# A two-layer decoder trunk on one core: the expert loop rewritten, with two-pass matmuls for experts of at most 64 tokens

## The reference

```python
def moe_swiglu(h, w_router, w_gu, w_down):
    logits = (h @ w_router).astype(jnp.float32)
    top_vals, top_idx = lax.top_k(logits, TOP_K)
    gates = jax.nn.softmax(top_vals, axis=-1)
    comb = jnp.sum(jax.nn.one_hot(top_idx, N_EXPERTS, dtype=jnp.float32) * gates[..., None],
                   axis=-2).astype(h.dtype)
    y = jnp.zeros_like(h)
    for e in range(N_EXPERTS):
        y = y + comb[..., e:e + 1] * swiglu(h, w_gu[e], w_down[e])
    return y
```

## Time and profile before

| | before |
|---|---|
| median of 3 runs | 1827.52 us (1825.49 to 1830.34) |
| profiled execution, span | 1824.5 us |
| TensorE, VectorE, ScalarE busy | 1688.0, 1270.3, 1020.9 us |
| moved by DMA | 452.27 MB, mean 248 GB/s |
| expert stage | from the first gather at 632.84 us to the end |

### The profile page before, as it was taken

How to read it: one execution, slowest core, us unless ns; L and a number is a source line. 1 busy time by engine, 2 the same in 40 slices (tenths; PEclk the granted TensorE clock), 3 DMA queues, 4 the chain that set the end, 5 groups by cost and what they waited for, 6 DMA issues and landing times.

```text
span 1824.5 us, 21578 instructions
## 1 busy us (share of the span) xinstructions
PE 1688.0 (93%) x7605; PEld 1391.9 (76%) x7606; DVE 1270.3 (70%) x1081; ACT 1020.9 (56%) x883; POOL 9.6 (1%) x22
## 2 busy tenths in 40 slices
PE   7999999999997889979979979979998899799996
PEld 5887778887786778868868868868886688688785
DVE  6645644454697568868878878856654788788886
ACT  4344433433476367757757757644544577577674
POOL 0000000000000000000000000000000000000000
PEclk9999999999998799989989989989998999899999
DMA  9553455555421269979979979946665699799893
GB/s 350 193 199 111 143 189 194 185 192 180 167 96 44 79 230 370 348 252 369 350 254 369 349 255 374 333 164 228 223 215 177 222 378 340 257 368 349 318 367 135
DMA packets 191716, 452.27 MB, mean 248 GB/s; under 512 B 8492, under 2 KB 8892, under 8 KB 191420
## 3 DMA queue, kind: packets, MB, share of 16 engines
q1 hardware_dynamic: 189212, 445.35, 69.2%
q10 hardware_dynamic: 2336, 4.78, 0.7%
HBM read 449.06 MB, written 1.05 MB: 247 GB/s over the span
## 4 chain that ended last, share of the span: by engine, by line
PE 88%; DVE 7%; issue 3%; ACT 1%; DMA 0%; DVEq 0%; POOL 0%; SPq 0%; ACTq 0%; POOLq 0%
PE bank L1218 28%; PE bank L1219 28%; PE bank L1222 26%; DVE y L996 2%; DVE wlo L739 2%; PE bank L1374 2%; PE bank L1483 1%; PE bank L1484 1%; DMA raw<-in_ret_w_in 0%; DVE z L751 0%; PE bank L1464 0%; PE bank L1262 0%; ACT whi L414 0%; DVE res L1160 0%; PE bank L1442 0%
## 5 line engine op out<-in xcount | busy, mean ns | idle before, releaser
L739 DVE TENSOR_TENSOR wlo<-raw,whi 128x2048 fp32r<-128x2048 f32 x422 | 964.3, 2290 | 340.4 <-ACT whi L414 340.1
L414 ACT ACTIVATE whi<-raw 128x2048 fp32r<-128x2048 f32 x422 | 807.7, 1916 | 423.0 <-PE bank L1222 366.3
L1218 PE MATMUL bank<-whi,xh 128*128 128x512 f32 x1520 | 607.9, 400 | 83.4 <-issue 62.4
L1219 PE MATMUL bank<-wlo,xh 128*128 128x512 f32 x1520 | 601.0, 395 | 0.0
L1222 PE MATMUL bank<-whi,xl 128*128 128x512 f32 x1408 | 556.5, 395 | 0.0
L1218 PEld LDWEIGHTS bank<-whi,xh 128*128 128x128 f32 x1520 | 291.8, 192 | 146.6 <-issue 71.1
L1219 PEld LDWEIGHTS bank<-wlo,xh 128*128 128x128 f32 x1520 | 291.3, 192 | 59.1
L1222 PEld LDWEIGHTS bank<-whi,xl 128*128 128x128 f32 x1408 | 269.8, 192 | 57.7
L1218 PE MATMUL bank<-whi,hTh 128*128 128x512 f32 x616 | 242.3, 393 | 4.4 <-DVE hTl L921 2.5
L1219 PE MATMUL bank<-wlo,hTh 128*128 128x512 f32 x616 | 242.6, 394 | 0.0
L1222 PE MATMUL bank<-whi,hTl 128*128 128x512 f32 x560 | 218.6, 390 | 0.0
(11 more groups left out here) (184 smaller groups left out, 792.1 us busy)
## 6 DMA issues: line engine op xcount, KB each, us to landing
raw<-in_moe_w_gu SPq DMA_DIRECT2D x224, 1024.0 KB, 6.4
raw<-in_moe_w_down SPq DMA_DIRECT2D x112, 1024.0 KB, 6.6
raw<-in_ffn_w_gu SPq DMA_DIRECT2D x28, 1024.0 KB, 5.1
raw<-in_ret_w_in SPq DMA_DIRECT2D x24, 1024.0 KB, 6.0
raw<-in_ffn_w_down SPq DMA_DIRECT2D x14, 1024.0 KB, 4.9
raw<-in_conv_w_pw SPq DMA_DIRECT2D x12, 1024.0 KB, 5.0
raw<-in_ret_w_out SPq DMA_DIRECT2D x8, 1024.0 KB, 4.8
res<-in_x SPq DMA_DIRECT2D x2, 512.0 KB, 4.6
```

The costliest lines, as they stand in the source:

```text
L414: nc.scalar.activation(whi[base % SPLIT][:, :], raw[base % RAW][:, :], ACT.Copy).then_inc(hi_done, 1)
L739: nc.vector.tensor_tensor(wlo[base % SPLIT][:, :], raw[base % RAW][:, :], whi[base % SPLIT][:, :].bitcast(f32), ALU.subtract).then_inc(lo_ ...
L1218: nc.tensor.matmul(dst, ah, bh, start=start, stop=False)
L1219: last = nc.tensor.matmul(dst, ah, bl, start=False, stop=stop and al is None)
```

## The change

Forms are now decided by tile and by 64 tokens: an expert is (HALF_FULL), (FULL), (FULL, HALF_FULL) or (FULL, FULL), for up to 64, 128, 192 and 256 tokens. In a half-full tile the tokens stand twice in the tile, so that the slice across the boundary between high part and remainder (`xmix`, `hTmix`) holds 64 columns of each; up and down blocks take two matmuls with it (`half_product`), gates take three. The two halves are added by the turn (with `fold` in place of the identity) and by the scatter. ScalarE's `low`, VectorE's `fold` and the buffers `glow` and `ulow` are gone.

Each engine has one loop over all eight experts, whose body holds each form once: ACT and DVE with one or two tiles, TensorE with four kinds. Gather of the next expert's first tile comes ahead of the last down rows; its evacuation, the evacuation of the last result, the scatter and the accumulation come inside the next expert, the scatter between its gate and up blocks. For expert 0 these work on a result weighted by zero (column 0 of `comb`), and after the loop one scatter and one accumulation follow. A second tile is gathered ahead of the expert's gates, and scattered and accumulated (`accumulate2`) at its end. The gates of an expert no longer run ahead of the last down rows of the one before. GpSimd has four memsets more.

```diff
-        xh = at("xh", [P, DC, SEQ], f32r)
-        xl = at("xl", [P, DC, SEQ], f32r)
+        xx = at("xx", [P, DC, TILES, 2 * P], f32r)
+        xh, xl, xmix = xx[:, :, :, 0:P], xx[:, :, :, P:2 * P], xx[:, :, :, HALF:HALF + P]
...
+            nc.gpsimd.memset(zeros[:, :].bitcast(f32), 0.0).then_inc(moe_set, 1)
+            nc.gpsimd.memset(onehotT[:, :, :].bitcast(f32), 0.0).then_inc(moe_set, 1)
+            nc.gpsimd.memset(comb[:, :, 0:1], 0.0).then_inc(moe_set, 1)
+            nc.gpsimd.memset(slot[:, NE, :, :], -1.0).then_inc(moe_set, 1)
...
+            def expert(e, tiles):
+                six, done = STEPS * e, STEPS * e + STEPS
+                xh_gathered(e)
+                if tiles == 2:
+                    xh_gathered2(wide_before(act, e))
+                hi(B_MOE + 1, six)
+                y_hi(B_MOE + 6 * six)
+                hi(B_MOE + 2, six)
+                hi(B_MOE + 3, six)
+                silu(done, B_MOE + 2 + 6 * six, tiles)
+                hi(B_MOE + 4, six)
+                hi(B_MOE + 5, six)
+                ohT_evac(e, tiles)
+                with act.Fori(0, STEPS - 1) as i:
...
+                hTh_evac(done + STEPS, tiles)
+                if tiles == 2:
+                    y_hi2(B_MOE + MOE_BLOCKS + 6 * six)
...
             def build_onehot(e):
-                for i, (a, b) in enumerate(((0, P), (0, HALF), (HALF, P))):
-                    at_ = (0, P, P)[i]
-                    for t in range(TILES):
-                        last = nc.vector.tensor_scalar(onehot[:, t, at_ + a:at_ + b], iota[:, a:b],
-                                                       slot[:, i, t, bass.ds(e, 1)], None, ALU.is_equal)
+                for h in range(2):
+                    for n in range(2 * TILES):
+                        at_ = n % 2 * P + h * HALF
+                        last = nc.vector.tensor_scalar(onehot[:, n // 2, at_:at_ + HALF], iota[:, h * HALF:(h + 1) * HALF],
+                                                       slot[:, bass.ds(e, 1), n, h], None, ALU.is_equal)
...
+            def expert(e, tiles):
+                six, done = STEPS * e, STEPS * e + STEPS
+                n2 = wide_before(dve, e) if tiles == 2 else None
+                xl_gathered(e, tiles, n2)
+                lo(B_MOE + 1, six)
+                y_lo(e)
+                lo(B_MOE + 2, six)
+                lo(B_MOE + 3, six)
+                accumulate(e)
+                hidden(done, B_MOE + 4 + 6 * six, tiles)
                 dve.wait_ge(ohT_ps, e + 1)
                 build_onehot(e + 1)
...
                 lo(B_MOE + 4, six)
                 lo(B_MOE + 5, six)
+                with dve.Fori(0, STEPS - 1) as i:
+                    hTl_evac(done + 1 + i, tiles)
+                    for b in range(6, 10):
+                        lo(B_MOE + b, six + i)
+                    hidden(done + 1 + i, B_MOE + 8 + 6 * (six + i), tiles)
+                    lo(B_MOE + 10, six + i)
+                    lo(B_MOE + 11, six + i)
+                hTl_evac(done + STEPS, tiles)
+                if tiles == 2:
+                    y_lo2(n2)
+                    accumulate2(e, n2)
...
+            def half_product(dst, both, bh, bl, start, stop):
+                nc.tensor.matmul(dst, both, bh, start=start, stop=False)
+                return nc.tensor.matmul(dst, both, bl, start=False, stop=stop)
...
+            def expert(e, kinds):
+                six, done, tiles = STEPS * e, STEPS * e + STEPS, len(kinds)
+                gates = (FULL,) * tiles
+                n2 = wide_before(pe, e) if tiles == 2 else None
+                if tiles == 2:
+                    gather(e, 1).then_inc(gather2_ps, 1)
+                pe.wait_ge(xel_done, e + 1)
+                columns(B_MOE, bank[0:2], 0, kinds=gates, six=six)
+                columns(B_MOE + 1, bank[0:2], 1, kinds=gates, six=six)
+                pe.wait_ge(yl_done, e + 1)
+                scatter(0, SCAT).then_inc(scat_ps, 1)
+                pe.wait_ge(hTl_done, done)
+                columns(B_MOE + 2, bank[2:4], 0, kinds=kinds, six=six)
+                columns(B_MOE + 3, bank[2:4], 1, kinds=kinds, six=six)
+                pe.wait_ge(res_done, 2 * e + 8)
+                onehot_turn(tiles)
...
+                hT_turn(done, kinds)
+                with pe.Fori(0, STEPS - 1) as i:
...
+                pe.wait_ge(silu_done, done + STEPS)
+                pe.wait_ge(onehot_done, e + 2)
+                gather(e, 0).then_inc(gather_ps, 1)
+                pe.wait_ge(hTl_done, done + STEPS)
+                expert_rows(B_MOE + 40, 0, False, kinds, six)
+                expert_rows(B_MOE + 41, 2, True, kinds, six)
+                if tiles == 2:
+                    pe.wait_ge(y2l_done, n2 + 1)
+                    scatter(1, SCAT2).then_inc(scat2_ps, 1)
+                    pe.wait_ge(acc2_done, n2 + 1)
...
+            with pe.Fori(0, NE) as e:
+                need = need_of(pe, e)
+                with pe.If(need > 1):
+                    with pe.If(need > 2):
+                        expert(e, (FULL, FULL))
+                    with pe.Else():
+                        expert(e, (FULL, HALF_FULL))
+                with pe.Else():
+                    with pe.If(need > 0):
+                        expert(e, (FULL,))
+                    with pe.Else():
+                        expert(e, (HALF_FULL,))
+            pe.wait_ge(yl_done, NE + 1)
+            scatter(0, SCAT).then_inc(scat_ps, 1)
```

More of the change, by code:

```diff
@@ L36 @@
 PAD = TAPS - 1
[L37 removed]
+FULL, HALF_FULL = 1, 2
+MOE_BLOCKS = STEPS * STEP_BLOCKS
 HALF = P // 2
@@ L526, in step @@
-            def step(base, s, tiles, six=0, then=None, n=None, ahead=False):
-                if not ahead:
-                    hi(base, six)
-                    hi(base + 1, six)
-                hTh_evac(s, tiles)
+                for t in range(tiles):
+                    last = nc.scalar.activation(hTh[:, :, t, :],
+                                                bank[2 + t][:, :].rearrange("p (c n) -> p c n", c=4), ACT.Copy)
+                last.then_inc(hTh_done, 1)
+            def step(base, s, six):
+                hi(base, six)
+                hi(base + 1, six)
+                hTh_evac(s, TILES)
@@ L1212, in _ @@
+            y_lo(NE)
+            accumulate(NE)
             norm(4)
@@ L1488, in onehot_turn, with gather @@
-            def onehot_turn(e):
-                for s in range(2):
+            def gather(e, tile):
+                for c in range(DC):
+                    dst = bank[2 * tile + c // 4][:, c % 4 * P:(c % 4 + 1) * P]
+                    for t in range(TILES):
+                        where = onehot[:, t, tile * P:(tile + 1) * P]
+                        nc.tensor.matmul(dst, zh[:, t, c * P:(c + 1) * P], where, start=t == 0, stop=False)
+                        last = nc.tensor.matmul(dst, zl[:, t, c * P:(c + 1) * P], where, start=False, stop=t == TILES - 1)
+                return last
```

606 lines of the change are left out of this document (233 added, 373 removed).

## The result

The changed kernel takes 1782.57 us (median; 1780.6 to 1783.2), the kernel before 1826.51 beside it. The ratio is 0.9752, with a 95% interval of 0.9738 to 0.9765. The forecast was 1810: the sign was right, but the gain, 2.5%, is more than twice the forecast 1%.

A forecast was written before the change was run, and what follows sets the result against it. One-tile steps were taken as TensorE-bound at 16.87 us, DMA close behind at 16.3, with instruction stalls between experts. Start, eight experts, jumps and end summed to 1807.3 us of span; 3.0 more gave 1810, range 1748 to 1850.

The forecast's parts named there:

- Instruction stalls: TensorE between experts: 12 us before a small expert, 10.5 before a middle or wide one; exits 3.2 (middle), 5.3 (wide).
- The price by distance: TensorE's jumps beyond the pages held cost about 5.3 us each (3.3 to 6.8), two far ones 10.5.
- Rival 1: TensorE's buffer keeps pages over the loop, so all entry stalls but the first go, 91 us: time 1719; chance 12%.
- ScalarE and VectorE: Their instruction stalls between experts should go, but lie beside TensorE's and so gain nothing.
- Small experts: Two passes cut TensorE's step from 16.87 to 13.2 us; the step becomes DMA-bound at 16.3 us.
- My count of VectorE's step: VectorE in a one-tile step: six lo at 2.2 us and two evacuations of 0.6 us make 14.4 us.
- The base of 112.8 us: Small expert from gates to end without jumps: lo 4 wait, load, 29 blocks x 2.71 us, conversion and last rows.
- Middle experts: Blocks stay TensorE-bound: 128.9 us without jumps, 142.6 with them, against 137.3 in the kernel before.
- The wide one: Expert 4: steps of 30.2 us with a third gate pass, serial gather and end work; 235.7 us without jumps.
- Start and end: First gates at 644.4 us (638.9 before), with 3.4 us for the gather; 14.2 us remain after the last rows.
- Rival 2: Instruction fetches queue behind weights after small experts; doubled cost at nine jumps adds 48 us: 1858; chance 18%.
- Rival 3: Small experts' steps don't get shorter, held by weight transfers or split-buffer waits: 1830 us, no change; chance 15%.

The follow-up runs named there:

- written-out steps: Changed kernel with TensorE's inner loop over the six steps written out for the one-tile forms, same matmuls in the same order: 1864.54 us.
- with more distance: Changed kernel with 817 more TensorE instructions in the branch (FULL, FULL) that no expert of this input enters: 1783.64 us.
- without the unused form: Changed kernel with the form (FULL, FULL), which no expert of this input enters, taken out on TensorE: 1744.85 us.
- the kernel before without its unused form: Kernel before with the never-entered form for two full tiles taken out on all three engines: 1775.53 us; on TensorE alone 1810.42.
- reordered kernel: Changed kernel with VectorE's lo 4 put before hidden and lo 5 before the one-hot work in one-tile steps: 1757.71 us.
- the rewrite with three passes: Changed kernel with the plan's threshold moved so every expert's first tile takes three passes over gate and up weights: 1836.37 us.

## Why the prediction was half right

Its own sum against the trace, from first gates to first gates (expert 4 from its second gather):

| stretch | forecast | measured | difference |
|---|---|---|---|
| up to expert 0 | 644.4 | 648.0 | +3.6 |
| expert 0, small | 124.8 | 117.8 | -7.0 |
| expert 1, small | 123.3 | 115.3 | -8.0 |
| expert 2, middle | 142.6 | 129.2 | -13.4 |
| expert 3, middle | 142.6 | 133.3 | -9.3 |
| expert 4, wide | 253.0 | 258.0 | +5.0 |
| expert 5, small | 124.8 | 123.5 | -1.3 |
| expert 6, small | 124.8 | 122.0 | -2.8 |
| expert 7 and end | 127.0 | 134.2 | +7.2 |
| sum | 1807.3 | 1781.4 | -25.9 |

The miss of 25.9 us is the smaller part of what went wrong: 62 us too much were charged for instructions, and 36 too little for the rest (24 in the small experts, 6 in the wide one, 3.6 at the start, 1.4 at the end, under 1 in the middle ones). That the total came out within 1.5% is partly luck.

**Instruction stalls: the step that failed.** I charged 91.2 us for jumps inside the experts' part. Measured as idle time are 3.9, 5.3, 3.8 and about 16 of the 18.98 us at 1401.67 (accumulate2 of the wide expert had ended near 1385.6): 29 us, and none at experts 1, 2 and 3. With all but the first entry's gone the kernel took 37.7 us less. The price by distance is refuted: 817 instructions more between the jumps changed nothing, and the written-out steps cost 82 us, with fetches also where the code runs straight on. Rival 1, to which I gave 12%, had the mechanism, though not the size (1719 us, against 1744.9 measured with the stalls gone), since it overlooked that the wide expert's own code drives the small form's out. It also put the reason against it wrongly: that only adjacent pages are shown kept. The trace of before had the sign that I needed. A working set just above what is kept looks the same at the seam as one with no keeping at all; the number of fetches, 92 in all, for a loop run seven times over seven to nine pages and the next ones behind them, fits with both, and only a kernel with fewer pages tells them apart.

The Trainium skill (Runtime: NRT & Kernel Launch, Instruction fetch mechanics), on which the forecast leaned, says that a taken branch outside a window of two pages stalls for a fetch. The runs disagree for TensorE: jumps of six to twelve pages cost nothing at experts 1 to 3. The same section's 2,048 instructions for TensorE, eight pages, agree with them. Counted with the next page behind each that is touched, the one-tile experts that run free of stalls have seven or eight (the changed kernel, with more distance, without the unused form) and eight or nine (the kernel before without its unused form); those that stall have nine to eleven (the kernel before, the written-out steps).

**ScalarE and VectorE: right for a wrong reason.** The forecast said that their stalls go and gain nothing, as they lie beside TensorE's. With TensorE's gone they are what holds the seam: 6.79 to 7.61 us at experts 1, 2, 3 and 5, and 1810.4 us in place of 1775.5. The rows had a sign of it: the text on record counts the 11.11 us at 1212.88 among six stalls for instructions, but the earlier trace rows give that wait, and the 3.30 us at 1698.95, to lo.

**Small experts.** The step was put at 16.3 us from the 386 GB/s of the earlier trace rows; it is 15.13, set by VectorE. My count of VectorE's step, 14.4 us, took 2.2 us for each lo, 4.4 for two, where two take 4.40 to 4.60 from start to start here, and left out the wait of 0.43 us. The base of 112.8 us came out 2.5 and 5.0 us too small in experts 1 and 0 all the same, and 5.4 to 5.8 in experts 5 to 7 (their stalls taken off), though each step saved 1.2 us. Lo 4 isn't the reason: it came 17.8 us behind the first gates in expert 0 (648.01 to 665.78) and 15.6 in expert 1, where the sum has 17.6 (15.4 and one lo). What is missing lies behind it, 100.1 and 99.8 us in place of 95.2. TensorE restarts there at half clock, and the gather of 3.6 us (758.52 to 762.12) stands between the last transposes and the last rows, for which the sum of a small expert had no term. How the rest divides isn't shown. The reordered kernel got the wait and the half clock back: there an expert takes 113.

**Middle experts.** 128.9 us forecast without jumps, 129.2 measured. **The wide one.** Forecast 235.7 without jumps; measured 258.0 less about 16 us, 242; the kernel without the unused form, which doesn't stall there, takes 242.6 (1135.62 to 1378.19). Its steps were right (30.2 forecast, 30.5 measured); the ends cost 6 to 7 us more.

**Start and end.** The gather started at 634.97, about as counted, but at half clock it took 6.8 us and not 3.4, and the gates began at 648.0. The last part has 15.6 us behind expert 7, 14.2 forecast.

**Rivals 2 and 3.** Rival 2, a fetch behind queued weights, has one case for it: the four fetches between 1386 and 1399 us for expert 5, some 16 us. But the DMA share from 1368 to 1400 is only 0.31, so it isn't load that makes them slow; it is four in a row. Rival 3 is out: the steps got 1.7 us shorter.

**Where the 43 us of span come from.** Read as a path over measured kernels: from before (span 1824.5) without its unused form (1772.3) to the rewrite with three passes (1831.4) to the changed kernel (1781.4). Keeping the pages is worth -52.2, the rest of the rewrite +59.1, two passes -50.0. Between the second and third kernel, by the transposes that open each expert: +6.2 up to expert 0, +3.7 over experts 0 to 2, +34.2 over 3 and 4, +12.9 over 5 and 6, +2.1 at the end. The wide expert's serial second gather and scatter and its third gate pass are the largest part, its eviction of the others' pages the next. The moved gather and scatter alone weren't tried, so their share isn't shown.

## What to carry to other kernels

Count the pages of code that one turn of a loop executes on each engine, and hold that against the number of fetches in the profile: if each turn fetches, take out or merge forms until it doesn't, on all engines at once, since stalls side by side cost their longest and curing one shows nothing. A long branch that is seldom taken is dear twice, by its own fetches and by those of the forms that it drives out. And when TensorE's work is cut, give the freed time away deliberately: the converting engine's order at the seam decides when the next load can start.

## What the runs showed of the hardware

- TensorE keeps pages of 256 instructions that it has executed over a loop's return: no fetch from 681 to 1140 us in the changed kernel, through three returns and three far jumps. A loop of at most seven pages had no stall behind its first expert (1744.9 us), although some pages were still fetched. Which page goes when a new one comes isn't settled. By the queue's rows in short windows, the starts of experts 5, 6 and 7 behind the wide one still had four, three and two fetches, though each of these small experts touches four to six pages; if the least recently used page went, expert 6 would have needed none.
- Code that must wait for its page waits about 4 to 5 us: 3.83 us at expert 7, where one fetch begins just ahead of the wait, 5.34 us at expert 6 with two inside it, and about 16 at expert 5 for four in a row, 12.6 more than the same seam takes without them.
- A wait of 2.34 to 2.84 us in a TensorE that is else busy is followed by some microseconds of half clock: the granted clock is 0.92 over 895.0 to 916.6 us of the changed kernel, 1.00 over the same step of the reordered one.
- ScalarE's and VectorE's code behaves alike with a smaller unit, 8 KB per fetch (0.08 MB in 10): 76 fetches in the kernel before, 14 without its unused form, with waits of 11.14 and 6.31 us at a seam in the one and no wait of either engine that ends in "issue" from 640 us on in the other.
- The expert weights' transfers ran at 394 to 396 GB/s where they bound the steps, above the 386 of the earlier trace rows; a step may run faster for a while, on the lead in the raw slots.
